# Layer 1's modulation: five groups of four 512-column slabs as 2048-column slabs

## What is computed

```python
def adaln(cond, w_ada, b_ada):
    mod = jax.nn.silu(cond) @ w_ada + b_ada
    return jnp.split(mod, N_MOD, axis=-1)      # sh1, sc1, g1, sh2, sc2, g2

def modulate(h, shift, scale):
    return h * (1.0 + scale) + shift

for i in range(DEPTH):                          # DEPTH = 2
    sh1, sc1, g1, sh2, sc2, g2 = [m[:, None, :] for m in adaln(c, w_ada[i], b_ada[i])]
    hl = modulate(rmsnorm(xl), sh1, sc1)
    yl = attention(hl, ...) if i == 0 else short_conv_mixer(hl, ...)
    xl = xl + g1 * yl
    xl = xl + g2 * conv_ffn(modulate(rmsnorm(xl), sh2, sc2), ffn_w_up[i], ffn_conv[i], ffn_w_down[i])
return rmsnorm(xl, final_gain)
```

## Time and profile before

| | us |
|---|---|
| median of 3 runs | 2725.49 (2724.74 to 2732.68) |
| the profiled execution, whole | 2727.95 |
| its span in the profile (first to last instruction) | 2726.3 |
| PE busy in the span | 2608.7 (96%) |
| DVE busy | 2030.7 (74%) |
| ACT busy | 1290.5 (47%) |

### The profile page before, as it was taken

How to read it: one execution, slowest core, us unless ns; L and a number is a source line. 1 busy time by engine, 2 the same in 40 slices (tenths; PEclk the granted TensorE clock), 3 DMA queues, 4 the chain that set the end, 5 groups by cost and what they waited for, 6 DMA issues and landing times.

```text
span 2726.3 us, 42805 instructions
## 1 busy us (share of the span) xinstructions
PE 2608.7 (96%) x14306; PEld 2195.2 (81%) x14306; DVE 2030.7 (74%) x2724; ACT 1290.5 (47%) x1730; POOL 244.7 (9%) x349
## 2 busy tenths in 40 slices
PE   6999999998979999999999899999899999999998
PEld 3666788876868888888888788888788888888887
DVE  5676988676778988888666688778888767775543
ACT  4322233477645554545444444445455555554443
POOL 1000222000001111011000011001111000000000
PEclk8999999999989999999999999999999999999998
DMA  8774988433668888888787789778688666665553
GB/s 313 263 248 159 301 272 268 123 93 131 221 195 260 271 265 257 270 265 275 240 252 255 247 250 292 246 246 267 211 270 258 217 187 192 185 192 185 184 182 127
DMA packets 471789, 622.82 MB, mean 228 GB/s; under 512 B 19540, under 2 KB 404982, under 8 KB 470672
## 3 DMA queue, kind: packets, MB, share of 16 engines
q1 hardware_dynamic: 424256, 450.94, 49.9%
q0 software_dynamic: 47120, 170.51, 21.8%
q10 hardware_dynamic: 320, 0.13, 0.0%
HBM read 619.41 MB, written 2.10 MB: 228 GB/s over the span
## 4 chain that ended last, share of the span: by engine, by line
PE 67%; DVE 14%; DMA 8%; issue 6%; ACT 4%; DVEq 1%; SPq 0%; ACTq 0%; POOLq 0%; POOL 0%
PE ps L1673 34%; PE ps L1675 17%; DMA ada_ring<-in_w_ada_dram 7%; PE ps L1663 4%; DVE ada_sum L1052 4%; DVE w_lo L992 4%; PE ps L1664 2%; PE ps L1548 2%; PE ps L1604 2%; PE ps L1605 2%; PE ps L1606 2%; ACT w_hi L513 1%; PE ps L1615 1%; DVE part_a L1219 1%; DMA first_x<-in_w_ada_dram 1%
## 5 line engine op out<-in xcount | busy, mean ns | idle before, releaser
L1673 PE MATMUL ps<-xs,w_hi 128*128 128x512 f32 x3840 | 1363.4, 400 | 48.5 <-DVE w_lo L992 26.4
L513 ACT ACTIVATE w_hi<-raw 128x1024 fp32r<-128x1024 f32 (+1 forms) x800 | 829.1, 1040 | 808.5 <-PE ps L1675 481.7
L992 DVE TENSOR_TENSOR w_lo<-raw,w_hi 128x1024 fp32r<-128x1024 f32 (+1 forms) x800 | 955.2, 1200 | 334.2 <-ACT w_hi L513 332.6
L1675 PE MATMUL ps<-xs,w_lo 128*128 128x256 f32 x3840 | 1074.0, 280 | 0.0
L1673 PEld LDWEIGHTS ps<-xs,w_hi 128*128 128x128 f32 x3840 | 724.1, 189 | 231.6 <-DVE w_lo L992 33.3
L1675 PEld LDWEIGHTS ps<-xs,w_lo 128*128 128x128 f32 x3840 | 726.8, 189 | 3.3 <-issue 3.1
L1673 PE MATMUL ps<-act,w_hi 128*128 128x512 f32 x1408 | 495.8, 397 | 0.0
L1675 PE MATMUL ps<-act,w_lo 128*128 128x256 f32 x1408 | 394.7, 280 | 0.0
L1052 DVE SCALAR_TENSOR_TENSOR ada_sum<-ada_ring,cond,ada_sum 128x512 f32<-128x512 f32 x455 | 341.2, 750 | 44.4 <-DMA ada_ring<-in_w_ada_dram 34.5
L431 POOL DMA_DIRECT2D ada_ring<-in_w_ada_dram x264 | 191.1, 724 | 1398.5 <-DVE ada_sum L1052 1345.6
L1673 PEld LDWEIGHTS ps<-act,w_hi 128*128 128x128 f32 x1408 | 264.2, 188 | 63.0
(11 more groups left out here) (200 smaller groups left out, 2428.3 us busy)
## 6 DMA issues: line engine op xcount, KB each, us to landing
raw<-in_ffn_w_up_dram SPq DMA_DIRECT2D x352, 512.0 KB, 4.7
ada_ring<-in_w_ada_dram POOLq DMA_DIRECT2D x264, 512.0 KB, 4.8
raw<-in_ffn_w_down_dram SPq DMA_DIRECT2D x128, 512.0 KB, 4.0
raw<-in_attn_w_qkv_dram SPq DMA_DIRECT2D x96, 512.0 KB, 5.1
raw<-in_sconv_w_in_dram SPq DMA_DIRECT2D x96, 512.0 KB, 5.3
raw<-in_ffn_w_down_dram SPq DMA_DIRECT2D x64, 384.0 KB, 3.3
ada_ring_kv<-in_w_ada_dram POOLq DMA_DIRECT2D x40, 512.0 KB, 6.0
raw<-in_attn_w_o_dram SPq DMA_DIRECT2D x32, 512.0 KB, 4.7
```

Source lines behind the costliest of these rows:

```text
L513: nc.scalar.activation(w_hi[:, slot, 0:n_tiles, :], raw[:, slot, 0:n_tiles, :], ACT.Copy).then_inc(hi_made, 1)
L992: nc.vector.tensor_tensor(w_lo[:, slot, 0:n_tiles, :], raw[:, slot, 0:n_tiles, :], w_hi[:, slot, 0:n_tiles, :], ALU.subtract).then_inc(lo_ ...
L1673: mm(ps[:, bank + m, :], w_hi[:, slot, t, cols], src[:, tile + t, :], start=(is_first and t == 0), stop=False)
L1675: last = mm(ps[:, bank + m, 0:T], w_lo[:, slot, t, cols], src[:, tile + t, 0:T], start=False, stop=(is_last and t == n_tiles - 1))
```

## The change

Of layer 1's 24 slabs (16 to 39) all but G1's four become five broad slabs of 2048 columns: a broad slab is one whole vector (SC1, SH1, SC2, SH2, G2). Its chunk is one row of tiles by 2048 columns, 1 MB, in a ring of two slots of 8 KB per partition (`broad_ring`, with `broad_sum` behind it, in memory that the attention leaves free and `act` fills only from up0's eighth body on). One DVE instruction of 2048 columns adds it; 16 chunks make a slab, at every 2.5th unit (`broad_at`), and 16 ones-matmuls reduce it.

Where they stand: broad slabs 0 and 1 in up0's bodies 1 to 3 and 4 to 6, the layer-0 slabs 13 to 15 (512 columns, as before) in its bodies 7 to 9, nothing in bodies 0 and 10; G1's four slabs in dn0, as numbers 16 to 19, at the same units of dn0 as its four before; broad slabs 2 and 3 in sin, over two bodies each, from the fifth unit on; nothing in so; broad slab 4 in up1's bodies 1 to 3. The one 512-column slab of stage o is as before. The broad chunks are issued by POOL, in the order of use, the first of slabs 0 and 1 after the norm before up0, of 2 and 3 after PE's last unit of dn0, of 4 after the norm before up1. Loops around the broad slabs are written out: up0's three bodies of a slab stand once in a loop of two, sin's four bodies and up1's three stand one after the other.

```diff
-ADA_AT = {"k": 4, "o": 12, "up0": 13, "dn0": 24, "sin": 28, "so": 34, "up1": 36}
+ADA_AT = {"k": 4, "o": 12, "up0": 13, "dn0": 16}
+
+BROAD_AT = {"up0": 0, "sin": 2, "up1": 4}
+BROAD_COLS = (SC1 * P, SH1 * P, SC2 * P, SH2 * P, G2 * P)
+BROAD_VECS = (B1 + SC1_1, B1 + SH1_1, B1 + SC2_1, B1 + SH2_1, B1 + G2)
...
-            body(0, True)
-            with eng.Fori(1, ADA_UP[phase]) as i:
-                body(i, True)
-            if ADA_UP[phase] < FT // 4:
-                with eng.Fori(ADA_UP[phase], FT // 4) as i:
-                    body(i, False)
+            body(0)
+            if phase == "up0":
+                with eng.Fori(0, 2) as g:
+                    for third in range(3):
+                        body(3 * g + (third + 1), broad=(g, third))
+                with eng.Fori(7, 10) as i:
+                    body(i, ada=i + (ADA_AT["up0"] - 7))
+                body(10)
+            else:
+                for third in range(3):
+                    body(third + 1, broad=(BROAD_AT["up1"], third))
+                with eng.Fori(4, 11) as i:
+                    body(i)
+
+        def broad_at(n):
+
+            return next((t for t in range(16) if t * 5 // 2 == n), None)
 
 
...
+            def broad_slab(b):
+                for t in range(16):
+                    wait(pool, broad_step, 16 * b + t - 1)
+                    pool.dma_start(broad_ring[:, t % 2, :], ada_w[1][:, t, BROAD_COLS[b]:BROAD_COLS[b] + D]).then_inc(broad_full[t % 2], 16)
+            def slabs(layer, first_slab, end, col):
                 with pool.Fori(first_slab, end) as j:
                     ada_slab(j, layer, j * ADA_COLS + (col - first_slab * ADA_COLS))
+            slabs(0, ADA_AT["o"], ADA_AT["o"] + 1, (ADA_FIRST + ADA_AT["o"]) * ADA_COLS)
+            pool.wait_ge(sq_added, 8)
+            broad_slab(0)
+            broad_slab(1)
+            slabs(0, ADA_AT["up0"], ADA_AT["dn0"], (ADA_FIRST + ADA_AT["up0"]) * ADA_COLS)
+            slabs(1, ADA_AT["dn0"], ADA_AT["dn0"] + 4, G1 * P)
+            pool.wait_ge(w_used, UNITS["sin"])
+            broad_slab(2)
+            broad_slab(3)
+            pool.wait_ge(sq_added, 24)
+            broad_slab(4)
...
+            def broad_chunk(b, t):
+                ve.wait_ge(broad_full[t % 2], 128 * b + 16 * (t // 2 + 1))
+                w, scalar = broad_ring[:, t % 2, :], cond[:, 0, t:t + 1]
+                if t == 0:
+                    nc.vector.tensor_scalar(broad_sum[:, :], w, scalar, None, ALU.mult).then_inc(broad_step, 1)
+                else:
+                    ve.wait_ge(broad_step, 16 * b + t)
+                    nc.vector.scalar_tensor_tensor(out=broad_sum[:, :], in0=w, scalar=scalar, in1=broad_sum[:, :],
+                                                   op0=ALU.mult, op1=ALU.add).then_inc(broad_step, 1)
+            def broad_add(b):
+                ve.wait_ge(broad_reduced, b + 1)
+                v = vec[:, BROAD_VECS[b]:BROAD_VECS[b] + 16] if isinstance(b, int) else vec[:, bass.ds(16 * b + BROAD_VECS[0], 16)]
+                nc.vector.tensor_tensor(v, v, ps[:, 7, 0:16], ALU.add).then_inc(broad_added, 1)
...
                                     g_point(k, phase, 2 * i + p, 0)
                                 n = 8 * p + 4 * h + k
-                                if ada:
-                                    j = i + ADA_AT[phase]
-
-                                    if n == 3 and first(i, p + h):
-                                        ada_chunk(j, 2)
-                                    if n < 8 and not (n == 2 and first(i, p + h)):
-                                        ada_chunk(j, n)
+                                if ada is not None:
+                                    if n < 8:
+                                        ada_chunk(ada, n)
                                     if n == 14:
-                                        ada_add(j)
+                                        ada_add(ada)
+                                if broad is not None:
+                                    m = n + 16 * broad[1]
+                                    if broad_at(m) is not None:
+                                        broad_chunk(broad[0], broad_at(m))
+                                    if m == 45:
+                                        broad_add(broad[0])
...
-                        ada_in_24("sin", i, 4 * n + k)
-            pair_loop(ve, sin_six)
+                        m, b = 24 * (i % 2) + 4 * n + k, BROAD_AT["sin"] + i // 2
+                        if broad_at(m - 4) is not None:
+                            broad_chunk(b, broad_at(m - 4))
+                        if m == 47:
+                            broad_add(b)
+            for i in range(4):
+                sin_six(i)
...
-                        n = 8 * i + 4 * h + k
-                        if n in (16, 31):
-                            ada_add(ADA_AT["so"] + n // 31)
-                        for q in range(16):
-                            if q % 8 * 13 // 8 + 16 * (q // 8) == n:
-                                ada_chunk(ADA_AT["so"] + q // 8, q % 8)
-            for i in range(4):
-                so_pair(i)
+            loop(ve, 4, so_pair)
...
+            def broad_reduce(b):
+                pe.wait_ge(broad_step, 16 * b + 16)
+                for t in range(16):
+                    last = mm(ps[:, 7, t:t + 1], broad_sum[:, P * t:P * t + P], ones[:, 0:1], start=True, stop=True)
+                last.then_inc(broad_reduced, 1)
 
...
-                                if ada and 4 * g + k == 8:
-                                    ada_reduce(i + ADA_AT[phase])
+                                if ada is not None and 4 * g + k == 8:
+                                    ada_reduce(ada)
+                                if broad is not None and 16 * broad[1] + 4 * g + k == 39:
+                                    broad_reduce(broad[0])
```

64 lines of the change are left out of this document (22 added, 42 removed).

## The result

| | us |
|---|---|
| kernel before, median of 5 runs | 2731.79 (2724.74 to 2732.9) |
| changed kernel, median of 5 runs | 2703.91 (2698.7 to 2710.21) |
| ratio, changed to before | 0.9905, 95% interval 0.9882 to 0.9929 |
| profiled execution, before and after | 2727.95 and 2699.41 |
| ratio in a second series (7 runs against 14) | 0.9907, interval 0.9879 to 0.9934 |

The change makes the kernel about 1% faster: 26 us by the ratio, 28.5 us between the two profiled executions. The prediction was 2699 with a range from 2687 to 2720: the median of this series is 5 us above it, that of the second series, 2699.44, on it.

What follows compares the result with a forecast made beforehand. PE, busy 96% of the span, was taken as the bound, so only its waits counted; 26.2 + 1.9 + 0 - 2 = 26.1 us off 2727.95 gave 2701.9 profiled, 2699 as median, range 2687 to 2720.

Steps and rivals of the forecast that it cites:

- Term 1: PE's waits for `w_lo` in up0, sin and up1's start: 26.2 us gained, bounds about 4 and 29.2.
- the six stretches: up0's first body, bodies 1 to 6, 7 to 9 and 10, sin, up1's start: 33.1 us of PE's `w_lo` waits.
- they stay: up0's bodies 7 to 9 are left as they are, so their 3.9 us of waits stay.
- Term 2: Norms before up0 and sin, no longer held by sums: 1.9 us gained, bounds 1.0 and 2.7; nothing at up1's.
- Term 3: Ones-matmul reductions on PE: same total cost before and after, zero, give or take 2 us.
- Term 4: PE's own pace, 2.77 or 2.80 us a unit: 2 us lost, bounds 5 us gain and 6 loss.
- The first: Rival: in up's nine broad bodies the long sum delays ACT and DVE, 2.3 us wait each; 2717 us, chance 0.12.
- The second: Rival: the DMAs become the bound in up0's bodies 1 to 6, sin, up1's 1 to 3; 2739 us, chance 0.09.
- the prediction's doubt: Whether DMAs carry 340 GB/s in broad slabs: 95% full by the skill's page, 80% by the trace's 424 GB/s.
- The third: Rival: PE's slower pace, 2.80 instead of 2.77 us, spreads over all 576 units from up0 to up1; 2714 us, chance 0.07.

Runs made afterwards that it cites:

- the small chunks: The changed kernel with most broad chunks loading 512 of their 2048 columns, a quarter of the bytes; 2703.91 us (one run).

## Why the prediction held, step by step

**Term 1, the waits**, was forecast at 26.2 us and brought 24.2: in the six stretches has 33.1, after there are 2.8 + 5.9 + 0.2 = 8.9. The long sum's price was right (2346 ns by a forecast of 2.3 to 2.4), and the broad bodies waited 3.0 us in all, where 3 were forecast. That hit is luck: 1.2 us are the branch back over the two-pass loop, 1.6 us a late transfer, and hardly anything is the sum of lags that I worked out. Bodies 7 to 9 have the same code as before and wait 5.9 us, not 3.9. In the eight profiles with this code they wait from 2.2 to 5.9 us, so "they stay" is not refuted and the 2 us are chance. Spread over eleven units these waits are gone.

**Term 2, the norms**, was forecast at 1.9 us and brought 3.7 by the first unit of each stage: up0's from 16.55 to 13.81 us above a usual unit (2.7), sin's from 15.33 to 14.23 (1.1), up1's from 13.16 to 13.26. Both halves came about otherwise than I reasoned.

At up0's norm I misread. The `w_hi` at 766.39 is the fourth unit's, and the fourth `w_lo` stands right behind the residual before and after. The third `w_lo` (768.50) belongs to a `w_hi` that was ready at 762.18 + 1.06 = 763.24, so it was held not for 1.0 us but by all the sums ahead of it. In the kernel before:

```profile
762.18 1.06 ACT L513 ACTIVATE w_hi<-raw 128x1024 fp32r<-128x1024 f32 x1 [1.71 <-PE ps L1675]
...
769.63 0.68 DVE L1129 TENSOR_TENSOR y<-y,ps 128x512 f32<-128x512 f32 x1
...
771.15 1.22 DVE L992 TENSOR_TENSOR w_lo<-raw,w_hi 128x1024 fp32r<-128x1024 f32 x1
771.94 1.35 PEld L1686 LDWEIGHTS ps<-part_c,ones 128*128 128x128 f32 x4 [5.69 <-ACT part_c L591]
```

In the changed kernel the three `w_lo` follow each other, then the addition, the residual and the fourth `w_lo`:

```profile
761.75 3.49 DVE L1030 TENSOR_TENSOR w_lo<-raw,w_hi 128x1024 fp32r<-128x1024 f32 x3
765.16 0.68 DVE L1165 TENSOR_TENSOR y<-y,ps 128x512 f32<-128x512 f32 x1
...
766.67 1.22 DVE L1030 TENSOR_TENSOR w_lo<-raw,w_hi 128x1024 fp32r<-128x1024 f32 x1
...
767.47 0.73 PEld L1729 LDWEIGHTS ps<-part_c,ones 128*128 128x128 f32 x4 [3.10 <-ACT part_c L629]
```

PE's last unit of o ends at 765.80 before and at 763.91 after, so the second half of the sum of squares begins 6.14 us behind it before and 3.56 after: 2.6 us won, in place of 1.0. All ten profiles with broad slabs have it at 3.5 to 3.6.

At sin's norm the sums gave next to nothing: the same matmuls begin 3.19 us behind dn0's last unit before, 3.05 after. The 1.1 us are in the main the granted clock, which is low around every norm, for 13.7 us here before and for 10.2 after. The 18.1 us from the end of dn0 on, before and then after:

```profile
1554.95:1573.05 18.10, 7.43 (x26) 5.50 (x25) 15.70 (x27) 9.90 (x19) 1.45 (x2) 0.62 0.53 169
```

```profile
1539.20:1557.30 18.10, 7.62 (x32) 5.98 (x31) 14.63 (x27) 10.45 (x21) 1.10 (x2) 0.72 0.56 200
```

It changes from execution to execution. In the seven of the ten profiles in which the clock was low for 13.7 us at sin's norm, the first unit ends 17.7 to 18.0 us behind dn0, against 18.1 before; in the three with 10.2 us, 17.0 to 17.3. At up0's norm it is 17.2 to 17.5 and 15.9 to 16.6 us, five profiles each, against 19.3 before, where the clock was low for 13.7. So some 2 us of term 2 stand in every profile, near the forecast's 1.9, but nearly all of them at up0; the rest is luck.

**Term 3, the reductions**, is the mis-sized one. Forecast 0 give or take 2 us, it cost 7.6: the units at the five broad reductions hold 5.02 + 3.58 + 5.15 + 6.65 + 5.14 = 25.5 us above a usual unit, where 5 x 3.58 = 17.9 were reckoned, and rightly, for the matmuls themselves. I priced sixteen as four times four; the trace of before held the hint, in the eight ones-matmuls at 245.26 and behind its longest wait for `w_lo` in sin, where PE's loads run slow as well:

```profile
1691.00:1695.00 4.00, 2.24 (x13) 1.72 (x12) 3.35 (x5) 1.06 (x1) 0.72 (x1) 1.00 0.75 256
1695.10:1698.50 3.40, 3.40 (x13) 2.92 (x12) 3.37 (x4) 1.06 (x1) 0.72 (x1) 0.50 0.91 248
```

I read that as part of the wait (2.08 us). A stretch in which PE idles or runs one-column matmuls has to be priced with what the clock may do behind it. The page "TensorE: Matmul & The Clock Gate" of the Trainium skill says in its part 1 (What's actually happening) that the low clock is the default and activity releases it, and ties a fall back to it to PE being idle; the rows agree with the first, and add that PE need not be idle: at 935.60 it was busy 3.70 of 3.70 us.

**Term 4, the pace**, was forecast at -2 and came to +0.5 over all. Its price was misread too: in the stretch of the earlier trace rows every unit takes 2.82 or 2.83 us from end to end, and 2.80 comes from counting the matmuls at both edges of the window. A slow unit costs 0.054 us, not 0.03. By stage: in up0, sin and up1 195 units run at 2.83 us where 146 did (49 x 0.054 = -2.7 us), in dn0 and so 3.2 us were won the same way (61 slow units to none). It is where the time of single executions moves most, as three experiments showed, and it was rightly kept as a bound rather than a forecast.

**The sum** was 26.1 us; by stage the parts that the change touches gave 25.0, the ratio 26. It came out because several misses cancel, which is luck: less from term 1 (-2.0) and term 3 (-7.6), more from term 2 (+1.8), term 4 (+2.5), and two items that the sum had not: the low clock behind the wait in sin is gone too (+1.5), and the units with a wait had been longer than the wait's own row by what is left (+2.7). A total within 1 us of the forecast does not prove the terms.

**The rivals.** The first, that the long sum holds up more than DVE, fell: no broad body waits 2.3 us for it, and cutting it to 64 columns gave PE 5 us. The second, the DMAs as the bound, fell with the small chunks, and the chunks of 1 MB were never late for DVE. Most of the first broad slab shows it as well:

```profile
826.00:930.00 104.00, 104.00 (x590) 90.14 (x589) 100.75 (x107) 53.62 (x71) 7.97 (x15) 1.00 0.93 322
```

PE is busy in all 104.00 us at 322 GB/s. That is 90% of the about 358 GB/s that raised the prediction's doubt (the Trainium skill's page "DMA: Bandwidth & Descriptors", Specifications), so no limit of that size was met here. The third, the slower pace everywhere, fell in up1 and holds in sin, where 90 of 96 units are slow; it cost 1.1 us there against before, since 69 were slow already. With 0.054 us a unit its full price would have been 31 us, not 17.

**What code costs in fetching** I took at nothing, since no row prices it. The branch back of the two-pass loop, whether by fetching or otherwise, costs 1.2 us of PE's time by 3.4 us of DVE's. DVE's waits for a chunk and the reductions' own waits (none of either) came as forecast, and ACT's waits for `raw` did not grow (87 us before, 88 after). Two signs were missed: PE's waits for `w_lo` are 10.1 us where near 7 were forecast, and up0's bodies 1 to 3 and 4 to 6 take 140.4 and 141.4 us, not 138, in part by PE's slower pace and the low clock.
